# Weights and streamed operands of TensorE placed 64 bytes apart, modulo 128, in a decoder layer

## What is computed

```
h = rmsnorm(x, norm_mix);  proj = h @ w_in                       # 1024 x 5656
q_a, kv_a, g_a, qkv_b, g_m = split(proj)
y_a = nsa_attention(...)                                         # 8 heads, three branches
y_b = dilated attention, groups (128,1),(512,4),(2048,16), merged by softmax denominators
merged = sigmoid(gate_a) * (y_a @ w_up_nsa) + sigmoid(gate_b) * (y_b @ w_up_dil)
x = x + merged @ w_out
h = rmsnorm(x, norm_ffn)
gt, up = split(h @ w_ffn_in)                                     # 1024 x 5632
x = x + (silu(gt) * up) @ w_ffn_out                              # 2816 x 1024
out = rmsnorm(x, norm_final)
```

## The kernel before

| operand | address before | modulo 128 |
|---|---|---|
| `n_hi`, `n_lo` (later `m`), and `a`, `y` | A, A + 45056, E | 0 |
| `w_raw`, `w_hi`, `w_lo`, weight sums | B and slots of 8960 bytes | 0 |
| `h_hi`, `h_lo` | Dd, Dd + 16384 | 0 |
| `t_hi`, `t_lo` | C, A + 45056 | 0 |
| `wa_hi0` / `wa_lo0` | Dd + 32768 / H + 8192 | 0 / 64 |
| `wa_hi1` / `wa_lo1` | H / H + 14464 | 64 / 64 |
| the four `wa22` tiles | G + 4608 and on | 0 |

## Time and profile before

### The profile page before, as it was taken

The page is one execution under the profiler, slowest core; times in us unless marked ns, Lnnn a source line. Parts: engine busy times, 40 slices in busy tenths (PEclk is TensorE's granted clock), DMA queues, the critical chain, the costliest instruction groups (busy, mean ns, idle before and its releaser), DMA issues.

```text
span 783.5 us, 12585 instructions
## 1 busy us (share of the span) xinstructions
PE 775.8 (99%) x4994; PEld 676.3 (86%) x4994; DVE 485.5 (62%) x920; ACT 327.2 (42%) x597; POOL 154.6 (20%) x111
## 2 busy tenths in 40 slices
PE   9999999999999999999999999999999999999996
PEld 7878899889878787788888988999999999888885
DVE  5935432555776767656625668898788876332347
ACT  5212055254446666653313624444444443222145
POOL 1300100000000000002200185876666650000000
PEclk9999999999999999999999999999999999999999
DMA  6941336250311111036331731334333335333302
GB/s 217 339 154 54 108 61 155 57 167 4 109 54 55 55 55 41 23 98 190 108 108 54 229 94 55 108 109 117 104 104 107 108 109 192 130 108 107 107 1 107
DMA packets 101286, 83.50 MB, mean 107 GB/s; under 512 B 16960, under 2 KB 94832, under 8 KB 101232
## 3 DMA queue, kind: packets, MB, share of 16 engines
q1 hardware_dynamic: 100992, 82.46, 35.2%
q10 hardware_dynamic: 240, 0.29, 0.1%
HBM read 77.44 MB, written 5.29 MB: 106 GB/s over the span
## 4 chain that ended last, share of the span: by engine, by line
PE 99%; DMA 0%; ACT 0%; DVE 0%; issue 0%; ACTq 0%; DVEq 0%
PE bank L1681 28%; PE bank L1682 28%; PE bank L1683 28%; PE bank L1914 2%; PE bank L1933 2%; PE bank L1901 2%; PE bank L1815 1%; PE bank L1856 1%; PE bank L1837 1%; PE bank L1778 1%; PE bank L1722 1%; PE bank L1705 1%; PE bank L1728 1%; PE bank L1928 1%; PE bank L1731 0%; PE bank L1868 0%
## 5 line engine op out<-in xcount | busy, mean ns | idle before, releaser
L1028 DVE TENSOR_TENSOR w_lo<-w_raw,w_hi 128x2048 fp32r<-128x2048 f32 (+2 forms) x29 | 64.5, 2224 | 79.5 <-ACT w_hi L677 79.4
L1681 PE MATMUL bank<-n_hi,w_hi 128*128 128x512 f32 x272 | 108.8, 400 | 0.0
L1683 PE MATMUL bank<-n_hi,w_lo 128*128 128x512 f32 x272 | 106.1, 390 | 0.0
L1682 PE MATMUL bank<-n_lo,w_hi 128*128 128x512 f32 x272 | 106.0, 390 | 0.0
L677 ACT CAST w_hi<-w_raw 128x2048 fp32r<-128x2048 f32 (+2 forms) x29 | 53.6, 1848 | 61.8 <-PE bank L1683 51.1
L1681 PE MATMUL bank<-w_hi,a_hi 128*128 128x512 f32 (+1 forms) x180 | 69.3, 385 | 0.0
L633 POOL TENSOR_TENSOR n_lo<-merge_tmp,n_hi 128x512 fp32r<-128x512 f32 x8 | 10.4, 1298 | 298.2 <-ACT n_hi L859 298.2
L1682 PE MATMUL bank<-w_lo,a_hi 128*128 128x512 f32 (+1 forms) x180 | 69.2, 384 | 0.0
L1683 PE MATMUL bank<-w_hi,a_lo 128*128 128x512 f32 (+1 forms) x180 | 69.2, 384 | 0.0
L1681 PE MATMUL bank<-w_hi,n_hi 128*128 128x256 f32 (+2 forms) x192 | 62.1, 323 | 0.0
L1683 PE MATMUL bank<-w_hi,n_lo 128*128 128x256 f32 (+2 forms) x192 | 61.4, 320 | 0.0
(11 more groups left out here) (268 smaller groups left out, 1927.4 us busy)
## 6 DMA issues: line engine op xcount, KB each, us to landing
w_raw<-in_w_ffn_in_dram SPq DMA_DIRECT2D x44, 512.0 KB, 5.0
w_raw<-in_w_in_dram SPq DMA_DIRECT2D x37, 512.0 KB, 4.9
w_raw<-in_w_ffn_out_dram SPq DMA_DIRECT2D x22, 512.0 KB, 4.2
w_raw<-in_w_out_dram SPq DMA_DIRECT2D x8, 512.0 KB, 4.1
w_raw<-in_w_in_dram SPq DMA_DIRECT2D x12, 256.0 KB, 4.7
xs<-in_x_dram SPq DMA_DIRECT2D x4, 512.0 KB, 4.6
wck_k<-in_w_ck_dram SPq DMA_DIRECT2D x1, 2048.0 KB, 11.8
wck_v<-in_w_cv_dram SPq DMA_DIRECT2D x1, 2048.0 KB, 15.0
```

The costliest lines, as they stand in the source:

```text
L1028: dve.tensor_tensor(wlo[u % 2][:, 0:n], raw[u % 2][:, 0:n], whi[u % 2][:, 0:n].bitcast(F32), ALU.subtract).then_inc(lo_done, 1)
L1681: pe.matmul(dst, w[0], x_[0], start=start, stop=False)
L1682: pe.matmul(dst, w[0], x_[1], start=False, stop=False)
L1683: return pe.matmul(dst, w[1], x_[0], start=False, stop=stop)
```

## The change

It moves tiles, and issues the same instructions on the same engines in the same order. B and all that is counted from it (C, Dd, G) move up by 64 bytes; H ends at remainder 0; `h` and `t_hi` get 64 bytes more of their own; `wa_hi0` moves from behind `h` to A + 61504, and the other `wa` blocks and four small tiles are set so that they neither overlap nor keep the old remainder. An unused tile (`tanh_g`) goes, and `gate_mul` shrinks to the one row that was used.

```diff
-        B = Fo + 10240
+        B = Fo + 10240 + 64
-        nbias = [at("nsa_bias0", [2, S], H + 14464), at("nsa_bias1", [2, S], E + 16384)]
+        nbias = [at("nsa_bias0", [2, S], H + 14400), at("nsa_bias1", [2, S], E + 16384)]
-        rrow = at("rrow", [S], H + 12288)
+        rrow = at("rrow", [S], H + 12352)
-        rhalf = at("rhalf", [2, TT], H + 14368)
+        rhalf = at("rhalf", [2, TT], G + 17536)
-        hhi, hlo = (at(f"h_{k}", [KC, S], Dd + o, F32R) for k, o in (("hi", 0), ("lo", 16384)))
+        hhi, hlo = (at(f"h_{k}", [KC, S], Dd + 64 + o, F32R) for k, o in (("hi", 0), ("lo", 16384)))
-        tg = at("tanh_g", [2, S], A + 61440)
-        tm = at("gate_mul", [2, S], A + 65536)
+        tm = at("gate_mul", [1, S], A + 65600)
-        gs = at("gate_scaled", [2, S], H + 4096)
+        gs = at("gate_scaled", [2, S], H + 4160)
         ahi7 = [[at(f"wa_hi{j}", [KC, P], o, F32R), at(f"wa22_hi{j}", [4, P], o2, F32R)]
-                for j, o, o2 in ((0, Dd + 32768, G + 4608), (1, H, G + 8704))]
+                for j, o, o2 in ((0, A + 61504, G + 4608), (1, H + 64, G + 8704))]
         alo7 = [[at(f"wa_lo{j}", [KC, P], o, F32R), at(f"wa22_lo{j}", [4, P], o2, F32R)]
-                for j, o, o2 in ((0, H + 8192, G + 6656), (1, H + 14464, G + 10752))]
+                for j, o, o2 in ((0, H + 8256, G + 6656), (1, H + 14400, G + 10752))]
-        thi = at("t_hi", [4, 4, 256], C, F32R)
+        thi = at("t_hi", [4, 4, 256], C + 64, F32R)
```

## The result

The changed kernel takes **790.20 us** (median of 4 runs, 789.94 to 790.53), the kernel before 783.83 (783.56 to 784.01) beside it: a ratio of 1.0082, interval 1.0064 to 1.0099. It is slower by 6.4 us, where 10.4 us less were forecast.

What follows compares the result with a forecast made beforehand. The prediction took TensorE, by the distance between matmul starts, to bound the kernel. Gains of 7.7 + 1.9 + 0.6 + 0.2 = 10.4 us off the 783.8 us median gave 773.4 us, range 768 to 779.

Steps and rivals of the forecast that it cites:

- step 4: The 1908 512-wide matmuls: no change taken, with ends of 12.7 us gained or lost.
- Step 1: 256-wide products of units 5 to 21: weights at the other remainder modulo 128 make matmuls 6.7 ns shorter, 7.7 us off.
- step 2: 256-wide matmuls of the value tiles: 24 go from 2.88 to 2.72 us, 1.9 us off.
- step 3: 256-wide matmuls of ffn_first, 0.6 us off, and the end of the second feed-forward product, 0.2 us off.
- the 512-wide matmuls begin to clash: Rival: at different remainders 512-wide stream and load meet once per matmul, at 233.3 ns; 12.7 us more, 786.1 us; chance 0.07.
- The even units' third: P1 in even unit 12, 1.41 us: two thirds of 12 matmuls at 120.0 ns, the third on wa_lo0 at 113.3.
- The exchange of the sides: Value tiles have n stationary and weights moving; the 1.9 us gain was assumed to hold that way round too.
- step 5: The 96 matmuls 280 wide: no change taken, ends 0.5 us either way.
- step 6: Transposes with ident and other matmuls, 220 in all: no change expected, ends 0.3 us either way.
- step 8: DMA writing w_raw at addresses shifted by 64: nothing taken, loss at most 1.2 us.
- Step 7: VectorE's L1476 may pay 0.07 us in odd units, hidden; about 0.75 us of slack per unit stays.
- No effect: Rival: addresses don't matter; something else that alternates, such as PSUM banks, makes the unit difference; 784 us, chance 0.04.

Runs made afterwards that it cites:

- experiment 2: Bare stream of matmuls on TensorE alone, each offset setting run behind two different streams; 256 wide, 192/192 took 113.3 ns and 64/64 117.8 ns behind both.
- experiment 3: Bare stream on TensorE alone, five weight settings behind four predecessors; 256 wide, 192/192 took 113.3 ns behind 256-wide runs and 117.8 behind the 512-wide one.
- experiment 6: Kernel before with only the seven products' weights in units 5 to 21 moved, high and low parts both to 192; median 777.73 us, ratio 0.9947.
- Experiment 4: Kernel before with only the seven products' weights in units 5 to 21 moved, high and low parts to 64 and 192; 777.84 us against 783.99.
- experiment 7: Experiment 4 plus ffn_first at 192/64 and the value tiles' moving weights 192 bytes up; 775.42 us, ratio to the kernel before 0.9895.
- experiment 1: Bare stream of split products on TensorE alone, 48 settings of byte offsets; 226.7 to 234.3 ns per matmul 512 wide, 113.3 to 120.0 ns 256 wide.

## Why the prediction was wrong

- **The sum** missed by 15.3 us between the profiled executions: 7.2 for step 4, 8.1 for steps 1 to 3.
- **Step 4 failed**: "I take nothing, because 226.7 is exactly twice 113.3". The exact doubling is real, and it says that 0/0 is the best place of a 512-wide stream. It says nothing of other places, and all that were tried cost 2.2 to 7.6 ns more. The rival "the 512-wide matmuls begin to clash" named the form, the direction and for `n` and `y` the size right (233.3 ns), and would have been +12.7; about half of the matmuls lie at 192 and pay only 2.2 ns. Its mechanism, a load and a stream that settle in a worse phase, is neither shown nor excluded by any run. Its point of decision, 5.5 ns a matmul, assumed that steps 1 to 3 hold. It got 0.07, though no row had a 512-wide matmul at different remainders.
- **Step 1 failed**: "only the stationary tile's remainder differs". The remainder modulo 128 was the change's own measure, not one that the trace had shown. Modulo 256 the buffers behind the 1.36 us lie at 192 for the high part and 64 for the low part; the change gives all of them 192. In the changed kernel that arrangement costs 117.8 ns: it takes the quick rhythm from odd P1 and P3, and gives the others 2.2 of the 6.7 ns. (192/192 can run at 113.3 too, experiments 2, 3 and 6. Here the products on `t` between them have the high part 64 from `t_lo`, a setting that the bare stream ran at 117.8 both times; that these hold P1, P3 and P7 in the slower rhythm is likely and not shown.) Experiment 4 shows that the size (6.8 of 7.7 us) and the mechanism were right, for the arrangement that the trace really held.
- **The even units' third** was read rightly: the single distances of unit 12's P1 before are close to 120, 121, 113, over and over, and the 113 follows the matmul on `wa_lo0`. But this tile lies at 192 modulo 256 and odd units' `wa_lo1` at 64, and the prediction took them for one case. After the change P1 has the same sum, 1.41 us, from twelve of about 117.8: two different rhythms that a sum of twelve doesn't tell apart.
- **Steps 2 and 3** got 0.6 of 1.9 and 0.3 of 0.8: value tiles and `ffn_first` lie at 192/192 too. The value tiles run at 117.8, and of `ffn_first` the first 24 matmuls run at 113.3 and the other 72, behind a single distance of 203 ns, at 117.8: both rhythms at one place within the changed kernel. The exchange of the sides, marked as not shown, did no harm: experiment 7 has 1.8 for the value tiles.
- **Steps 5, 6 and 8** hold: the 280-wide form moves by 0.02 us, with all other forms the sum is 0.0, and the landing of 256 KB takes 4.6 us against 4.7.
- **Step 7** holds for the time and not in its content. L1476 was to take 1.34 us; its successor L1475 takes 1.23 in both parities (below). Of VectorE's 0.76 and 0.49 us of waiting per unit, 0.55 is left in place of 0.75, though a unit is only 0.03 to 0.13 us shorter; the last section has the reason.
- **No effect** (the rule of two independent read ports) is out: experiment 1 varies the two operands' distance, with all other engines at rest. The Trainium skill, "SBUF — State Buffer" (Who interferes with whom), calls PE's two read ports independent; 226.7 against 233.3 ns, by the distance of what the two read, disagrees.

What in the chip makes the period of 256 bytes and the two rhythms is open; the runs give the map of costs alone, which shows that the distance is the cause and not how it acts.

## What to carry to other kernels

When an address is said to matter, write both operands' addresses out at more than one modulus, and check the claimed measure against every row that it should explain, high and low parts apart. Price a change of layout for each width of the stream: here the place that is best for 512 columns is the worst for 256, so here it paid to move the narrow forms alone (775.42 us against 790.20). And look at single start distances (113-113-114, 117-118-118, 231-236), as a sum of twelve hides which rhythm a run is in.

## What was not expected of the hardware

- One stream of 256 columns has two stable rhythms at the same addresses, 113.3 and 117.8 ns, and a pause or a short run at another place can switch it (experiments 2, 3 and 6, and `ffn_first` in the changed kernel). It lasts: in experiment 6 from unit 6 to the end of the stage.
- **VectorE and POOL collide, and timing alone decides who pays.** VectorE in the changed kernel, unit 11, then POOL:

```profile
552.69 0.70 DVE L1518 TENSOR_TENSOR bank<-bank,m_u_u 128x512 f32<-128x512 f32 x1
...
555.76 1.23 DVE L1475 TENSOR_TENSOR wa_lo<-w_raw,wa_hi 128x1024 fp32r<-128x1024 f32 x1 [0.24 <-ACT wa_hi L897]
...
558.48 3.48 DVE L1485 TENSOR_TENSOR w_lo<-weight_sums,w_hi 128x1024 fp32r<-128x1024 f32 x2
```

```profile
559.59 1.28 POOL L658 TENSOR_TENSOR weight_sums<-w_raw 128x512 f32<-128x512 f32 x1 [3.87 <-PE bank L1682]
560.95 2.15 POOL L660 TENSOR_TENSOR weight_sums<-weight_sums,w_raw 128x512 f32<-128x512 f32 x1
```

The same two lines in the kernel before, unit 11, VectorE and POOL:

```profile
553.79 2.35 DVE L1486 TENSOR_TENSOR w_lo<-weight_sums,w_hi 128x1024 fp32r<-128x1024 f32 x2
...
554.93 2.37 POOL L659 TENSOR_TENSOR weight_sums<-w_raw 128x512 f32<-128x512 f32 x1 [3.65 <-PE bank L1683]
```

Before, two of VectorE's took 2.35 us together, and POOL's L659, which started 0.01 us behind the second of them, took 2.37 in place of 1.28. After, POOL's starts 0.02 us ahead and VectorE's second one takes 1.1 us more (3.48 for the two), then POOL's L660 pays 0.9. That it is not the addresses is shown by unit 6 of the kernel before, where VectorE is the one that pays (2.31 us for L1486 at 497.58). In the 105 us from 547 on the mean of VectorE's line goes from 1217 to 1728 ns; this is nearly all of the 11.7 us of the stage window, and it eats the 0.76 us before L1519 (L1518 shows no wait above). It costs TensorE nothing here, and it is not what made the wait in unit 6 of experiment 4 longer, since VectorE's 2.31 us are there in both traces. The Trainium skill, "SBUF — State Buffer" (Who interferes with whom), describes a port pair that the two engines share as an exclusive lock, wanted by a VectorE instruction with two inputs in SBUF and by a POOL instruction that reads SBUF, with the order of issue deciding who blocks. The traces agree: whichever starts first takes its usual 1.22 or 1.28 us, and the other about 1.1 us more.
